# Experts to last embedding: a gate panel split ahead of the last copies, the embedding copied by VectorE, a semaphore for each mixed tile

## The reference

```python
x = x + hierarchical_moe(rms_norm(x, ffn_norm_g[i]), ...)        # top 2 of 32 experts, SwiGLU each
ple = rms_norm(p[i] @ w_ple[i], ple_norm_g[i])                   # p: 512 x 256, w_ple: 256 x 1024
x = x + jax.nn.sigmoid(rms_norm(x, ple_gate_norm_g[i]) @ w_ple_gate[i]) * ple
```

## Time and profile before

| | |
|---|---|
| three runs | 2184.66, 2186.82, 2188.53 us (median 2186.82) |
| the profiled execution | 2186.05 us, its span 2184.2 us, mean TensorE clock 0.991 of full speed |
| busy share of the span | PE 97%, DVE 58%, ACT 38%, POOL 13% |
| the chain that ended last | PE 75%, DVE 11%, DMA 6%, ACT 3%, issue 3%, POOL 2% |

### The profile page before, as it was taken

How to read it: one execution, slowest core, us unless ns; L and a number is a source line. 1 busy time by engine, 2 the same in 40 slices (tenths; PEclk the granted TensorE clock), 3 DMA queues, 4 the chain that set the end, 5 groups by cost and what they waited for, 6 DMA issues and landing times.

```text
span 2184.2 us, 27204 instructions
## 1 busy us (share of the span) xinstructions
PE 2122.5 (97%) x10482; PEld 1599.8 (73%) x10482; DVE 1271.1 (58%) x1689; ACT 833.9 (38%) x1252; POOL 283.8 (13%) x239
## 2 busy tenths in 40 slices
PE   8999999999999999999999999999999997999998
PEld 6787888888878877888788888877788883333346
DVE  7877855555587678874655555587674453000028
ACT  5556522222253445773422222364442332122143
POOL 2334200000010154000100000110000013232220
PEclk9999999999999999999999999999999989999999
DMA  5322322222214342213222222121132158999951
GB/s 195 112 88 90 116 96 96 89 109 90 91 67 156 119 147 77 45 30 116 105 110 86 98 103 86 67 77 59 58 124 89 61 213 327 400 403 388 392 223 59
DMA packets 62478, 298.13 MB, mean 136 GB/s; under 512 B 14064, under 2 KB 14448, under 8 KB 34310
## 3 DMA queue, kind: packets, MB, share of 16 engines
q1 hardware_dynamic: 41312, 258.49, 31.2%
q0 software_dynamic: 19824, 35.60, 5.3%
q10 hardware_dynamic: 1248, 2.76, 0.3%
HBM read 326.37 MB, written 22.48 MB: 160 GB/s over the span
## 4 chain that ended last, share of the span: by engine, by line
PE 75%; DVE 11%; DMA 6%; ACT 3%; issue 3%; POOL 2%; SPq 0%; ACTq 0%; POOLq 0%; DVEq 0%
PE psum L631 20%; PE psum L632 19%; PE psum L633 19%; PE psum L1356 4%; PE psum L1380 3%; DMA panel<-w_m 3%; PE psum L1066 2%; DVE a_lo L2044 2%; PE psum L1041 1%; DMA over_panel<-w_m,over_row 1%; DVE xc L2185 1%; DMA w_ple<-w_p 1%; ACT a_hi L1453 1%; DVE hs L2140 1%; PE psum L1168 1%
## 5 line engine op out<-in xcount | busy, mean ns | idle before, releaser
L631 PE MATMUL psum<-hn_hi,a_hi 128*128 128x512 f32 (+1 forms) x1592 | 626.9, 394 | 6.8 <-DVE hn_lo L2084 3.2
L633 PE MATMUL psum<-hn_hi,a_lo 128*128 128x512 f32 (+1 forms) x1592 | 619.1, 389 | 0.0
L632 PE MATMUL psum<-hn_lo,a_hi 128*128 128x512 f32 (+1 forms) x1592 | 618.8, 389 | 0.0
L631 PEld LDWEIGHTS psum<-hn_hi,a_hi 128*128 128x128 f32 (+1 forms) x1592 | 297.4, 187 | 78.8 <-issue 9.6
L633 PEld LDWEIGHTS psum<-hn_hi,a_lo 128*128 128x128 f32 (+1 forms) x1592 | 297.4, 187 | 64.5
L632 PEld LDWEIGHTS psum<-hn_lo,a_hi 128*128 128x128 f32 (+1 forms) x1592 | 297.4, 187 | 64.2 <-issue 2.2
L2044 DVE TENSOR_TENSOR a_lo<-a_raw,a_hi 128x2048 fp32r<-128x2048 f32 (+1 forms) x110 | 252.8, 2298 | 78.6 <-ACT a_hi L1453 78.1
L1453 ACT ACTIVATE a_hi<-a_raw 128x2048 fp32r<-128x2048 f32 (+1 forms) x110 | 205.2, 1867 | 79.7 <-PE psum L633 67.5
L2128 DVE TENSOR_TENSOR h<-h,psum 128x512 f32<-128x512 f32 x176 | 119.4, 687 | 78.4 <-PE psum L633 78.4
L3022 POOL TENSOR_TENSOR sq<-sq 128x512 f32<-128x512 f32 x6 | 9.0, 1507 | 1141.2 <-ACT sq L1466 1141.2
L2949 DVE TENSOR_TENSOR xhid<-xsg,psum 128x256 f32<-128x256 f32 x24 | 10.1, 421 | 242.8 <-ACT xsg L1994 242.8
(11 more groups left out here) (528 smaller groups left out, 3310.7 us busy)
## 6 DMA issues: line engine op xcount, KB each, us to landing
a_raw<-w_a SPq DMA_DIRECT2D x116, 1024.0 KB, 5.0
panel<-w_m SPq DMA_DIRECT2D x96, 1024.0 KB, 12.9
b_raw<-w_b SPq DMA_DIRECT2D x64, 512.0 KB, 3.3
q_scratch<-q_hi POOLq DMA_DIRECT2D x7, 384.0 KB, 3.4
q_scratch<-qb_lo POOLq DMA_DIRECT2D x7, 384.0 KB, 4.5
q_hi<-q_scratch POOLq DMA_DIRECT2D x7, 384.0 KB, 4.0
q_lo<-q_scratch POOLq DMA_DIRECT2D x7, 384.0 KB, 4.8
token_rows<-nat POOLq DMA_DIRECT2D x4, 512.0 KB, 4.5
```

Source lines behind the costliest of these rows:

```text
L631: pe.matmul(out, w_hi, x_hi, start=first, stop=False)
L632: pe.matmul(out, w_hi, x_lo, start=False, stop=False)
L633: return pe.matmul(out, w_lo, x_hi, start=False, stop=last)
```

## The change

Seven edits, all between the last expert step and the additions of the mixed tiles:

1. ScalarE: the split of the first gate panel and the loading of the Sqrt table stand right behind the last Silu, ahead of `copy_y(22)` and `copy_turned(23)`.
2. The last `copy_y` is halved: ScalarE copies bank 6, VectorE bank 7; each raises `y_copied`, and its waiters wait for one more.
3. The eight embedding tiles are copied to `ple` by VectorE, each after ScalarE's square of it.
4. The sums of the squares stand between these copies; the last addition stands behind the mixing.
5. ScalarE scales the first mixed tile ahead of the eighth square, the other three behind it.
6. The c = 1 gather of tile 0 has a semaphore of its own (`y_stored[0]`, which is free by then), so that each tile of the mixing waits for its own gathers.
7. SP no longer waits for all expert panels before the loads of gate panels three and four.

```diff
@@ SP
             load_a(A_PG)
             load_a(A_PG + 1)
-            sp.wait_ge(main_used, len(PANEL_ORDER))
             for p in range(2, 4):
                 load_a(A_PG + p)
@@ TensorE
             pe.wait_ge(ple_copied, KT)
-            pe.wait_ge(y_copied, NSTEP)
+            pe.wait_ge(y_copied, NSTEP + 1)
             keep(7, 10)
@@ ScalarE
                 if s + 2 < NSTEP:
                     window_a(s + 2)
+                if s == NSTEP - 1:
+                    high_a(A_PG)
+                    act.activation(warm[:, 6:7], eps, ACT.Sqrt)
                 if s:
                     copy_y(s - 1)
                     copy_turned(s)
-            copy_y(NSTEP - 1)
-            high_a(A_PG)
-            act.activation(warm[:, 6:7], eps, ACT.Sqrt)
+            act.wait_ge(*after_down(NSTEP - 1))
+            act.wait_ge(y_stored[1], 16 * (NSTEP // 2 - 1))
+            act.activation(y_out[:, 1, 0:512], bank[6][:, :], ACT.Copy).then_inc(y_copied, 1)
+
+            def scaled_back(t):
+                act.activation(back[:, t, 0, :], back[:, t, 0, :], ACT.Copy, scale=rt[:, 9, t:t + 1]).then_inc(back_scaled, 1)
+
             for m in range(KT):
                 act.wait_ge(ple_mm, m + 1)
                 square(T_PLE, m, bank[m % 4][:, :])
-                act.activation(ple[:, m, :], bank[m % 4][:, :], ACT.Copy).then_inc(ple_copied, 1)
-            act.wait_ge(back_loaded[0], 16 * (NT + 1))
-            for t in range(NT):
-                act.activation(back[:, t, 0, :], back[:, t, 0, :], ACT.Copy, scale=rt[:, 9, t:t + 1]).then_inc(back_scaled, 1)
+                if m == KT - 2:
+                    act.wait_ge(back_loaded[0], 16 * (NT + 1))
+                    scaled_back(0)
+            for t in range(1, NT):
+                scaled_back(t)
             high_a(A_PG + 1)
@@ VectorE
             low_a(A_PG)
+            V.wait_ge(*after_down(NSTEP - 1))
+            V.wait_ge(y_stored[1], 16 * (NSTEP // 2 - 1))
+            V.tensor_copy(y_out[:, 1, 512:1024], bank[7][:, :]).then_inc(y_copied, 1)
...
+            for m in range(KT):
+                V.wait_ge(sq_ready, KT * T_PLE + m + 1)
+                V.tensor_copy(ple[:, m, :], bank[m % 4][:, :]).then_inc(ple_copied, 1)
+                if 1 <= m <= 4:
+                    sums(T_PLE, [psq[:, k, :] for k in range(5)], [m])
+                if m == 6:
+                    V.tensor_tensor(psq[:, 5, :], psq[:, 5, :], psq[:, 6, :], ALU.add).then_inc(sq_total, 1)
...
             for t in range(NT):
-                V.wait_ge(back_loaded[max(t, 1)], 32 if t > 1 else 48)
+                if t:
+                    V.wait_ge(back_loaded[t], 32)
+                else:
+                    V.wait_ge(y_stored[0], 16 * (NSTEP // 2 + 1))
                 V.wait_ge(back_scaled, t + 1)
...
@@ GpSimd
-                        .then_inc(back_loaded[max(t, 1) if c else 0], 16)
+                        .then_inc((back_loaded[t] if t else y_stored[0]) if c else back_loaded[0], 16)
```

More of the change, by code:

```diff
@@ L2954, in _, with sums @@
             low_a(A_PG)
-            def sums(t, squares):
-                for k in range(1, 5):
+            V.wait_ge(*after_down(NSTEP - 1))
+            V.wait_ge(y_stored[1], 16 * (NSTEP // 2 - 1))
+            V.tensor_copy(y_out[:, 1, 512:1024], bank[7][:, :]).then_inc(y_copied, 1)
+            def sums(t, squares, ks=range(1, 5)):
+                for k in ks:
                     V.wait_ge(sq_ready, KT * t + k + 1)
@@ L2960, in sums @@
                     V.tensor_tensor(squares[0], squares[0], squares[k], ALU.add).then_inc(sq_summed, 1)
-            sums(T_PLE, [psq[:, k, :] for k in range(5)])
-            total(T_PLE)
+            for m in range(KT):
[5 more added lines that the diff above has]
+                    V.tensor_tensor(psq[:, 5, :], psq[:, 5, :], psq[:, 6, :], ALU.add).then_inc(sq_total, 1)
+                    V.wait_ge(sq_summed, 4 * T_PLE + 4)
+                    V.wait_ge(sq_total, 3 * T_PLE + 1)
+                    V.tensor_tensor(psq[:, 5, :], psq[:, 5, :], psq[:, 0, :], ALU.add).then_inc(sq_total, 1)
             for t in range(NT):
-                V.wait_ge(back_loaded[max(t, 1)], 32 if t > 1 else 48)
+                if t:
+                    V.wait_ge(back_loaded[t], 32)
+                else:
+                    V.wait_ge(y_stored[0], 16 * (NSTEP // 2 + 1))
                 V.wait_ge(back_scaled, t + 1)
@@ L2968, in _ @@
                                        ALU.mult, ALU.add).then_inc(mixed, 1)
+            V.wait_ge(sq_ready, KT * (T_PLE + 1))
+            V.wait_ge(sq_total, 3 * T_PLE + 2)
+            V.tensor_tensor(psq[:, 5, :], psq[:, 5, :], psq[:, 7, :], ALU.add).then_inc(sq_total, 1)
             V.wait_ge(back_mm, 1)
@@ L3109, in store_y @@
                 c = column(s)
-                pool.wait_ge(y_copied, s + 1)
+                pool.wait_ge(y_copied, s + 1 if s < NSTEP - 1 else NSTEP + 1)
                 pool.indirect_dma_start(
```

## The result

The changed kernel takes 2194.81 us (median of 10 runs, 2190.27 to 2198.01), the kernel before 2186.33 on the same chip (10 runs, 2184.66 to 2188.81): 8.5 us more, ratio 1.0038 with a 95% interval of 1.0029 to 1.0048. So it is slower, and by more than forecast: 2192.6 was the forecast, and the median lies at the very top of the range (2194.8), 0.01 over it.

What follows compares the result with a forecast made beforehand. It took a chain of waits through the last copy of y, store, gathers, mixing and transposes as the bound. The transposes' end moving +4.3 and the clock +1.5 made +5.8 us, so 2192.6 us, range 2188.0 to 2194.8.

Steps and rivals of the forecast that it cites:

- The wait for the load: ScalarE's early split stands at the first gate panel's load from 2094.36 to 2096.8; last down product starts 2.7 us late.
- The third rival: First gate panel lands in time for ScalarE's early split: +1.9 us, 2188.7, or 2190.2 with a clock fall; chance 0.17.
- The halved copy: Last copy of y split between ScalarE and VectorE: 0.33 us gained for the store and the gathers.
- VectorE's copies: Embedding copies on VectorE keep pace with TensorE's 1.75 us per tile; seven tiles cost nothing, the eighth is different.
- The eighth square: ScalarE's eighth square waits for the fourth gather and a scaling; last embedding copy done at 2122.5 instead of 2117.47.
- The tile semaphore: Tile 0's mixing waits only for the fifth gather, about 1.4 us; counted as nothing, covered by the late keep matmuls.
- The third panel's load: Issued about 2101 instead of 2107.6, out of the gathers' way: taken as 0, at most 1 us gained.
- The clock: TensorE's longer idle stretches before last down product and keep matmuls: 1.5 us for one fall, none for a second.
- Rival 1: Both clock falls on TensorE in full: +4.3 + 3.4 = +7.7 us, 2194.5; chance 0.18.
- late start: TensorE's last down product starts 2.7 us late, at 2101.5, because ScalarE delivers the turned rows late.
- first fall: TensorE's clock falls after 3.8 us of idling before the last down product: 1.5 us.
- second fall: TensorE's clock after the 3.4 us idle stretch before the keep matmuls: a fall there was taken as none.

Runs made afterwards that it cites:

- table_first: The changed kernel with the Sqrt table loaded ahead of the early panel split instead of behind it: 2191.95 us, ratio 1.0025.
- both_back_y_first: The changed kernel with split behind the last copy of y, all squares before scalings, and VectorE's half of y ahead of its split part: 2185.07 us, 0.9993.
- split_late: The changed kernel with the gate panel's split and Sqrt table put back behind the last copy of y: 2195.07 us, ratio 1.0046.
- both_back: The changed kernel with the split back behind the last copy of y and all squares ahead of the scalings: 2191.01 us, ratio 1.0031.
- best: The changed kernel with split behind the turned rows, y before a_lo on VectorE, squares before scalings, keep matmuls before the embedding wait: 2190.24 us, 1.0019.
- the two load_late runs: Gate panels three and four loaded after the mixing gathers: kernel before, 1.0000; both_back_y_first with keep matmuls before the embedding wait, 0.9996.
- only_split: The kernel before with only the panel's split and Sqrt table moved ahead of the copies of y(22) and turned rows: 2194.18 us, ratio 1.0035.
- filled: The changed kernel with eight matmuls that nobody reads in each of TensorE's two idle stretches: 2189.27 us, ratio 1.0022.
- square_first: The changed kernel with all scalings put back behind the eighth square: 2190.07 us, ratio 1.0026.

## Why the prediction came out as it did

**The wait for the load: right.** Forecast 2.4 us before the split and the down product 2.7 late; measured 2.60 and 7.65 − 4.79 = 2.86. Landing took 10.4 us after issue, as the earlier trace rows had it (10.2), and table_first confirms that it is the landing that decides. The third rival, a panel in time, is out: in every profile with an early split ScalarE waited, 1.13 us or more.

**The halved copy: right.** 0.33 forecast; both_back_y_first has its gathers 0.33 earlier. What I didn't see is that the half on VectorE hangs behind a_lo. In the changed kernel that costs nothing; it decides split_late and both_back. In best the half stands ahead of a_lo, and it is the load that a_lo releases that meets the store.

**VectorE's copies: right in sum.** Seven cost nothing; both_back_y_first is at 0.9993. The eighth costs the keep 0.51 there, and the sums between the copies go with the long issues of the gathers: in the changed kernel the fourth gather is issued 5.08 us behind the first, before 4.29. The prediction priced neither.

**The eighth square: right in mechanism and size.** Forecast: of the 5.03 by which the last copy of the embedding ends later (2122.5 against 2117.47), 2.7 are carried over and 2.33 are the gather and the scaling. Measured: it ends at +31.85, against +23.49 before; 5.71 of these 8.36 are the late and long down product, so 2.65 are the gather and the scaling. The 0.32 over the forecast are the gathers' own: the fourth landed 10.24 us after the first one's issue, before 9.89. The first four were issued 1.37 to 1.41 us long, where before they took 0.99, 0.95, 1.44 and 1.29.

**The tile semaphore: right.** Covered by the late keep: no transposes waited for a mixed tile, and 4.33 became 3.65 (I had 3.63).

**The third panel's load: right at 0 beside the gathers**, by the two load_late runs. It wasn't neutral where it met the last store. The changed kernel avoids that, and it is edit 7 that does it: only_split, with the early split and without edit 7, has its first gather 1.1 us later behind the store. The prediction didn't price that.

**The clock: the term that was mis-sized.** I took 1.5 us for one fall and nothing for a second. The profile has 6.50 − 3.65 = 2.85 at the down product and 7.09 − 4.42 = 2.67 at the keep (start to the first transpose), 5.5 together; filled gives 5.4 for both by taking them away. My measure of 1.7 was from the earlier trace rows, where the fall followed 2.59 us of idling and the clock was at 0.50 for 3.4 us. Here it was at 0.50 for 6.8 us each time; 5.8 and 5.4 of that lay over matmuls, and at half the clock these lose half of it. The mistakes were to let a single fall stand for the size of all, and to put the second at nothing. The prediction's only reason for that is that part of a fall can lie in an idle stretch; 1.0 and 1.4 of the 6.8 us did. Rival 1, both falls in full, is what happened, and at 2194.5 it stands nearer the median than my forecast. Its 3.4 is what the medians give (3.2) and too low for the profiled execution. The rise in the medians is 8.5 where I had 5.8; that the forecast in microseconds looks closer is partly luck, since the 2186.82 that it starts from lay 0.49 over the median of ten runs.

The steps in sum, forecast and measured, for the moment of the first addition: late start 2.7 and 2.86; first fall 1.5 and 2.85; the eighth square 2.33 and 2.65, net of the halved copy; second fall 0 and 2.67; transposes without waits −0.7 and −0.68. The forecast ones make the 5.8, the measured ones 10.35, against 10.34 in the whole. The Trainium skill (TensorE: Matmul & The Clock Gate, "What's actually happening") says that activity is what releases the throttled state; filled fits that, with a clock of 1.00 over both places once matmuls fill the idling.

## What to carry to other kernels

Before a step is moved ahead to fill an engine's idle time, look up when its input lands, last DMA engine and all, not when its buffer is free: a load that costs nothing behind three other steps costs its full rest ahead of them, and with it the time of whoever waits behind on that engine. Where the engine that waits is TensorE, price each idle stretch that the change makes longer twice, once as the wait and once as a clock fall of its own; here the falls cost 3.2 us in the medians and 5.4 in the profiled execution, beside some 5 for the waits. And when one copy is split over two engines, check what stands ahead of each half on its own engine.

## What the runs showed of the hardware

- What a clock fall cost was half of the time at 0.50 that lay over matmuls: of the first 6.8 us in the changed kernel 5.8 lay over the down product, which took 2.85 longer, and in square_first all of 3.4, for 1.70. The clock was at 0.50 for 3.4 us at a time in square_first, both_back, table_first and only_split, for 6.8 in the changed kernel and in best, and for 10.2 in split_late. The same sixteen matmuls took 6.50 us behind 3.92 us of idling, but 5.35 behind 2.45, 3.71 and 4.33; the same twenty took 7.25, 7.23 and 6.27 behind 3.81, 9.65 and 4.04. The 9.65 cost no more than the 3.81 because 4.8 of its 10.2 us at 0.50 lay in the idling. An idle stretch of 1.69 was followed by no fall in square_first, one of 1.85 by a fall in only_split. What decides how long a fall lasts no run here isolates.
- An indirect store of 128 rows landed 2.7 us after issue alone, and 4.1 (split_late) and 4.5 (both_back) beside a 1 MB load that SP had started 1.3 us earlier. Eight gathers of 4 MB didn't mind the same load.
- The first gate panel's 1 MB takes 10.1 to 10.8 us to land, although in before and in the changed kernel the sixteen DMA engines are busy to only 0.08 to 0.09 in its last microseconds; the third, issued once the other panels are in, took 4.7 to 5.3. What the late part of the first waits for no run here isolates.
- GpSimd's issue of an indirect transfer is long when it starts while VectorE runs an operation on two tiles in SBUF (a sum of squares, or a_lo). The 13 traces have 130 such issues between the last Silu and the last gather. The 80 that met none took 0.93 to 1.00 us, also those that met one of VectorE's copies from PSUM. The 50 that met one were longer by what that operation had left, less about 0.1 us: 0.48 left in before made 1.29, 0.60 left in the changed kernel 1.41, and the 1.42 of a_lo in best made 2.28. An operation that began only after the issue did not lengthen it (0.94 to 0.99, 24 times). No run changes this alone, so it is a match over 130 cases and not an experiment.
